# Second norm and its transposes moved, tile by tile, into the output product's second pass; the feed-forward opens with four half column tiles

## What is computed

```python
def rms_norm(x, g):
    y = x * rsqrt(mean(x * x, axis=-1, keepdims=True) + EPS)
    return y * g

def reference(x, ...):
    ...                                   # norm, combined projection, two attentions, gates -> merged
    x = x + merged @ w_out                # "output product", 1024 x 1024 x 1024
    h2 = rms_norm(x, g_mlp)               # "second norm"
    x = x + square(relu(h2 @ w_ff1)) @ w_ff2   # "feed-forward" (FF), 1024 -> 4096 -> 1024
    return x
```

## Time and profile before

| | |
|---|---|
| median of 3 runs | 1508.72 us (1506.99 to 1510.85) |
| profiled execution | 1510.88 us, of which its span is 1508.7 us |
| PE busy | 1447.4 us (96%), 7304 matmuls |
| PEld busy | 1209.2 us (80%) |
| DVE, ACT, POOL busy | 532.6, 363.2, 498.7 us |
| mean granted TensorE clock | 0.982 |

### The profile page before, as it was taken

The page is one execution under the profiler, slowest core; times in us unless marked ns, Lnnn a source line. Parts: engine busy times, 40 slices in busy tenths (PEclk is TensorE's granted clock), DMA queues, the critical chain, the costliest instruction groups (busy, mean ns, idle before and its releaser), DMA issues.

```text
span 1508.7 us, 18633 instructions
## 1 busy us (share of the span) xinstructions
PE 1447.4 (96%) x7304; PEld 1209.2 (80%) x7304; DVE 532.6 (35%) x974; ACT 363.2 (24%) x781; POOL 498.7 (33%) x351
## 2 busy tenths in 40 slices
PE   7999999976799999899998999999999999999998
PEld 6998888864488887788887888888888888888887
DVE  5300124078566665545235213222221322222222
ACT  5112120175355554200023102020110202011020
POOL 3331554117143241125405225060522406052320
PEclk9999999988799999999999999999999999999999
DMA  7120211000010000015202102030110203021012
GB/s 226 31 57 15 56 42 49 6 23 1 18 38 2 1 1 29 20 51 181 70 1 70 56 28 84 0 94 18 56 55 28 83 0 97 14 62 49 28 41 97
DMA packets 79285, 70.90 MB, mean 47 GB/s; under 512 B 7808, under 2 KB 70784, under 8 KB 79232
## 3 DMA queue, kind: packets, MB, share of 16 engines
q1 hardware_dynamic: 79088, 69.67, 15.2%
q10 hardware_dynamic: 144, 0.52, 0.1%
HBM read 65.99 MB, written 4.19 MB: 47 GB/s over the span
## 4 chain that ended last, share of the span: by engine, by line
PE 88%; DVE 4%; issue 3%; ACT 2%; POOL 1%; DMA 1%; ACTq 0%; SPq 0%; DVEq 0%; POOLq 0%
PE PS L986 73%; PE PS L1133 4%; PE PS L1179 4%; PE PS L993 2%; PE PS L1095 2%; PE PS L1152 1%; ACT scA L891 1%; DVE uT_lo L1623 1%; PE PS L1097 1%; POOL scA L681 1%; PE PS L1175 1%; PE PS L1159 1%; DVE x_norm L1584 0%; DMA x_in<-in_x 0%; PE PS L1148 0%
## 5 line engine op out<-in xcount | busy, mean ns | idle before, releaser
L571 POOL TENSOR_SCALAR w_hi<-raw 128x1024 fp32r<-128x1024 f32 x64 | 74.3, 1160 | 422.2 <-PE PS L986 412.3
L1623 DVE TENSOR_TENSOR uT_lo<-relu_sq,uT_hi 128x512 fp32r<-128x512 f32 x64 | 93.3, 1494 | 280.6 <-ACT uT_hi L974 280.6
L960 ACT ACTIVATE relu_t<-PS 128x512 f32<-128x512 f32 x64 | 34.8, 595 | 557.7 <-PE PS L986 557.7
L1629 DVE TENSOR_TENSOR xr<-PS,xr 128x1024 f32<-128x1024 f32 x64 | 78.4, 1225 | 245.7 <-PE PS L986 245.7
L573 POOL TENSOR_TENSOR w_lo<-raw,w_hi 128x1024 fp32r<-128x1024 f32 x64 | 158.8, 2482 | 5.3
L986 PE MATMUL PS<-w_hi,uT_hi 128*128 128x512 f32 x512 | 158.6, 391 | 1.7 <-DVE uT_lo L1623 1.7
L986 PE MATMUL PS<-h2T_hi,w_hi 128*128 128x512 f32 x512 | 159.2, 390 | 0.0
L986 PE MATMUL PS<-h2T_lo,w_hi 128*128 128x512 f32 x512 | 159.1, 389 | 0.0
L986 PE MATMUL PS<-h2T_hi,w_lo 128*128 128x512 f32 x512 | 159.0, 389 | 0.0
L986 PE MATMUL PS<-w_lo,uT_hi 128*128 128x512 f32 x512 | 157.9, 390 | 0.0
L986 PE MATMUL PS<-w_hi,uT_lo 128*128 128x512 f32 x512 | 157.7, 390 | 0.0
(11 more groups left out here) (194 smaller groups left out, 2395.4 us busy)
## 6 DMA issues: line engine op xcount, KB each, us to landing
raw<-in_w_ff SPq DMA_DIRECT2D x64, 512.0 KB, 3.7
g_raw<-in_w_in SPq DMA_DIRECT2D x16, 512.0 KB, 3.9
x_in<-in_x SPq DMA_DIRECT2D x8, 512.0 KB, 10.5
raw<-in_w_out SPq DMA_DIRECT2D x8, 512.0 KB, 3.5
xr<-in_x SPq DMA_DIRECT2D x8, 512.0 KB, 7.4
out<-xr SPq DMA_DIRECT2D x8, 512.0 KB, 2.6
z_raw<-in_w_in SPq DMA_DIRECT2D x4, 640.0 KB, 7.8
z_raw<-in_w_in SPq DMA_DIRECT2D x4, 544.0 KB, 4.0
```

What stands on the lines that cost most here:

```text
L571: pool.tensor_scalar(hi_ap, raw_ap, 1.0, 1.0, ALU.mult, ALU.mult).then_inc(hi_done, 1)
L960: act.activation(relu_t[:, cols], PS[:, 2 * (j % 2) + h, :], ACT.Relu).then_inc(relu_ready, 1)
L1623: dve.tensor_tensor(uT_lo[:, j, cols], relu_sq[:, cols], uT_hi[:, j, cols], ALU.subtract).then_inc(uT_ready, 1)
L1629: dve.tensor_tensor(xr[:, t, :], pair(4 + 2 * (t % 2)), xr[:, t, :], ALU.add).then_inc(x3_added, 1)
```

## The change

The second norm and its transposes go tile by tile into the second pass of the output product. After step n of the product, from n = 10 on, PE transposes the normalised tile n - 10 (`x2_transposes`), into banks 6 and 7; the second pass itself uses three pairs (0/1, 2/3, 4/5) in place of four (`out_pair`). Tile 5 follows the last step; tiles 6 and 7 stand inside the FF opening, `ff_begin`. Mean and power are now made for one tile at a time. The gain is multiplied in on DVE together with the normalisation, from `g_mlp_r`, the gain in all 128 rows (a 512 KB broadcast, issued by SP between the residual's loads and the output weights 4 to 7), where it was the scale of the copy out of PSUM. The copies out are `h2T_high` on ACT and `h2T_low` on DVE, two banks a tile, each 128 x 4 x 128, written over the part of `mT_hi`, `mT_lo` that belongs to the tokens just used (listings show them under the name `mT_`). ACT's squares go to `x_norm[:, t]` rather than to a scratch tile, so one squaring no longer waits for the one before. `ff_begin` does column tile 0 for tokens 0 to 511, tiles 6 and 7's transposes, column tile 1 for tokens 0 to 511, then both column tiles for tokens 512 to 1023. The small load of the gain by columns (`g_mlp_c`) at the start is gone.

```diff
@@ -369,6 +368,18 @@
             return t if c else t % 2
+        def out_pair(n):
+            return 2 * (n % 4) if n < T else 2 * ((n - 13) % 3)
+        def out_before(n):
+            return max([m for m in range(n) if out_pair(m) == out_pair(n)], default=None)
+        def x2_bank(t, a):
+            return (4 if t == T - 1 else 6) + a
         def bcast(ap, shape):
             return ap.to_broadcast(shape)
...
@@ -526,6 +536,8 @@
             sp.wait_ge(branch_done, 2 * KD)
             for t in range(T):
                 sp.dma_start(xr[:, t, :], x_d[t]).then_inc(xr_landed[t], 16)
+            sp.wait_ge(mT_ready, KD)
+            sp.dma_start(g_mlp_r[:, :], g_mlp[0:1, :].partition_broadcast(P)).then_inc(g_mlp_in, 16)
             for k in range(4, 8):
                 out_load(k)
...
@@ -741,10 +753,9 @@
                         split(raw[n % 2][:, :], w2_hi[j][:, :], w2_lo[j][:, :], w2_hi_done, 4 * g + j + 1, w2_ready)
                 unit(0, 1, 0)
                 if first:
-                    for h in range(2):
-                        pool.wait_ge(x2_ms_ready, h + 1)
-                        power(x_rstd[:, 4 * h:4 * h + 4], x_ms[:, 4 * h:4 * h + 4], 4, (P, 4)
-                              ).then_inc(x2_rstd_ready, 1)
+                    for t in range(T):
+                        pool.wait_ge(x2_ms_ready, t + 1)
+                        power(x_rstd[:, t:t + 1], x_ms[:, t:t + 1], 1, (P, 1)).then_inc(x2_rstd_ready, 1)
                 unit(1, 1, 1)
                 unit(2, 2, 0)
                 unit(3, 2, 1)
@@ -936,18 +947,22 @@
                 act.activation(mT_hi[:, d, :], merged[:, :], ACT.Copy).then_inc(mT_hi_done, 1)
+            def x2_square(t):
+                act.wait_ge(xr_added, T + t + 1)
+                act.activation(x_norm[:, t, :], xr[:, t, :], ACT.Square, accum_out=x_ss[:, t:t + 1]).then_inc(x2_squared, 1)
+            def h2T_high(t):
+                for a in range(2):
+                    act.wait_ge(x2T_done, 2 * t + a + 1)
+                    act.activation(h2T_hi[:, 4 * a:4 * a + 4, t * P:(t + 1) * P],
+                                   PS[:, x2_bank(t, a), :].rearrange("p (j q) -> p j q", q=P), ACT.Copy
+                                   ).then_inc(h2T_hi_done, 1)
             for t in range(T):
-                act.wait_ge(xr_added, T + t + 1)
-                if t:
-                    act.wait_ge(x2_squared, t)
-                act.activation(sq2[:, :], xr[:, t, :], ACT.Square, accum_out=x_ss[:, t:t + 1]).then_inc(x2_squared, 1)
-            for n in range(2 * KD):
-                h, j = n // KD, n % KD
-                act.wait_ge(x2T_done, n + 1)
-                if n == 0:
-                    act.wait_ge(o_done, 2 * T)
-                act.activation(h2T_hi[:, j, h * HALF:(h + 1) * HALF], PS[:, n % 8, :], ACT.Copy,
-                               scale=g_mlp_c[:, j:j + 1]).then_inc(h2T_hi_done, 1)
+                if t >= 2:
+                    h2T_high(t - 2)
+                x2_square(t)
+            h2T_high(T - 2)
+            h2T_high(T - 1)
             def ff_up(g, first):
...
@@ -1223,53 +1238,68 @@
             peeled(pe, KD // 2, branches)
-            for n in range(2 * T):
+            def out_tile(n):
                 r, t = n // T, n % T
                 if t == 0:
                     pe.wait_ge(mT_ready, 4 * (r + 1))
                 if n < 4:
                     pe.wait_ge(merged_ready, KD - 1 if n < 2 else KD)
-                if n >= 4:
-                    pe.wait_ge(xr_added, n - 3)
+                else:
+                    pe.wait_ge(xr_added, out_before(n) + 1)
                 rows = slice(t * P, (t + 1) * P)
                 for k in range(4 * r, 4 * r + 4):
                     if t == 0:
                         pe.wait_ge(ow_ready, k + 1)
+                    b = out_pair(n)
                     ins = split_products(mT_hi[:, k, rows], mT_lo[:, k, rows], ow_hi[k][:, :], ow_lo[k][:, :],
-                                         [(PS[:, 2 * (n % 4) + h, :], halves[h]) for h in range(2)],
+                                         [(PS[:, b + h, :], halves[h]) for h in range(2)],
                                          k, k == 4 * r, k == 4 * r + 3)
                 ins.then_inc(o_done, 1)
...
+            def x2_transposes(t):
+                pe.wait_ge(x2_normed, t + 1)
+                if t == 0:
+                    pe.wait_ge(xr_added, T)
+                elif t == T - 1:
+                    pe.wait_ge(xr_added, 2 * T)
+                else:
+                    pe.wait_ge(h2T_ready, 2 * t)
+                for a in range(2):
+                    transpose_tiles(x2_bank(t, a), [x_norm[:, t, j * P:(j + 1) * P] for j in range(4 * a, 4 * a + 4)]
+                                    ).then_inc(x2T_done, 1)
+            for n in range(2 * T):
+                out_tile(n)
+                if n >= T + 2:
+                    x2_transposes(n - T - 2)
+            def up_half(g, j, hs, ready=None):
+                pe.wait_ge(w1_ready, 4 * g + j + 1)
+                if ready is not None:
+                    pe.wait_ge(h2T_ready, ready)
+                for k in range(KD):
+                    ins = split_products(w1_hi[j % 2][:, k, :], w1_lo[j % 2][:, k, :], h2T_hi[:, k, :], h2T_lo[:, k, :],
+                                         [(PS[:, 2 * (j % 2) + h, :], halves[h]) for h in hs], k, k == 0, k == KD - 1)
+                return ins
+            def ff_begin():
+                pe.wait_ge(xr_added, 2 * T - 2)
+                up_half(0, 0, (0,), T)
+                x2_transposes(T - 2)
+                x2_transposes(T - 1)
+                pe.wait_ge(xr_added, 2 * T - 1)
+                up_half(0, 1, (0,))
+                up_half(0, 0, (1,), 2 * T).then_inc(up_done, 1)
+                up_half(0, 1, (1,)).then_inc(up_done, 1)
             def ff(g, first):
...
+                if first:
+                    ff_begin()
+                for j in range(2 if first else 0, GROUP):
+                    pe.wait_ge(relu_ready, 8 * g + 2 * j - 2)
+                    up_half(g, j, (0, 1)).then_inc(up_done, 1)
...
@@ -1579,10 +1609,21 @@
             peeled(dve, KD // 2, merge)
             def x2_norm(t):
-                if t % 4 == 0:
-                    dve.wait_ge(x2_rstd_ready, t // 4 + 1)
-                dve.tensor_scalar(x_norm[:, t, :], xr[:, t, :], x_rstd[:, t:t + 1], None, ALU.mult
-                                  ).then_inc(x2_normed, 1)
+                dve.wait_ge(x2_rstd_ready, t + 1)
+                dve.scalar_tensor_tensor(out=x_norm[:, t, :], in0=xr[:, t, :], scalar=x_rstd[:, t:t + 1],
+                                         in1=g_mlp_r[:, :], op0=ALU.mult, op1=ALU.mult).then_inc(x2_normed, 1)
+            def h2T_low(t):
+                for a in range(2):
+                    out = h2T_lo[:, 4 * a:4 * a + 4, t * P:(t + 1) * P]
+                    dve.wait_ge(h2T_hi_done, 2 * t + a + 1)
+                    dve.tensor_tensor(out, PS[:, x2_bank(t, a), :].rearrange("p (j q) -> p j q", q=P),
+                                      h2T_hi[:, 4 * a:4 * a + 4, t * P:(t + 1) * P], ALU.subtract).then_inc(h2T_ready, 1)
+            def x2_mean(t):
+                dve.wait_ge(x2_squared, t + 1)
+                dve.tensor_scalar(x_ms[:, t:t + 1], x_ss[:, t:t + 1], 1.0 / D, EPS, ALU.mult, ALU.add
+                                  ).then_inc(x2_ms_ready, 1)
             for n in range(2 * T):
@@ -1592,25 +1633,19 @@
                     dve.wait_ge(xr_landed[t], 16)
                 else:
                     dve.wait_ge(xr_added, T)
-                dve.tensor_tensor(xr[:, t, :], pair(2 * (n % 4)), xr[:, t, :], ALU.add).then_inc(xr_added, 1)
-                if r == 1 and t % 4 == 3:
-                    h = t // 4
-                    ts = slice(4 * h, 4 * h + 4)
-                    dve.wait_ge(x2_squared, 4 * (h + 1))
-                    dve.tensor_scalar(x_ms[:, ts], x_ss[:, ts], 1.0 / D, EPS, ALU.mult, ALU.add
-                                      ).then_inc(x2_ms_ready, 1)
-                if r == 1 and t in (5, 6):
-                    x2_norm(2 * t - 10)
-                    x2_norm(2 * t - 9)
-            for t in range(4, T):
-                x2_norm(t)
-            for n in range(2 * KD):
-                h, j = n // KD, n % KD
-                cols = slice(h * HALF, (h + 1) * HALF)
-                dve.wait_ge(h2T_hi_done, n + 1)
-                dve.scalar_tensor_tensor(out=h2T_lo[:, j, cols], in0=PS[:, n % 8, :], scalar=g_mlp_c[:, j:j + 1],
-                                         in1=h2T_hi[:, j, cols], op0=ALU.mult, op1=ALU.subtract
-                                         ).then_inc(h2T_ready, 1)
+                b = out_pair(n)
+                dve.tensor_tensor(xr[:, t, :], pair(b), xr[:, t, :], ALU.add).then_inc(xr_added, 1)
+                if r == 1:
+                    if t == 0:
+                        dve.wait_ge(g_mlp_in, 16)
+                    else:
+                        x2_norm(t - 1)
```

(33 more changed lines are left out.)

11 lines of the change are left out of this document (1 added, 10 removed).

## The result

| | before | after |
|---|---|---|
| first comparison, median of 5 runs each | 1508.72 us (1506.79 to 1511.13) | 1497.71 us (1495.93 to 1499.77) |
| ratio, 95% interval | | 0.9927 [0.991, 0.9945] |
| before once more, beside e1 to e4, 23 runs | 1506.25 us (1502.54 to 1510.98) | |
| profiled execution, span | 1510.88, 1508.7 us | 1497.08, 1495.1 us |
| mean granted clock of the profiled execution | 0.982 | 0.992 |

The change made the kernel faster, as forecast (1500.1 us, range 1497.5 to 1504.5), and it stands near the low end of the range. The first comparison gives 11.0 us.

A forecast was written before the change was run, and what follows sets the result against it. PE, holding 88% of the chain, bounds the kernel. Matmuls 21.76, transposes 6.96 and stall 0.95 make 29.67 us against 38.33, so 1508.72 - 8.66 = 1500.1 us; range 1497.5 to 1504.5.

The forecast's parts named there:

- The place: Between output product and FF, PE spends 16.47 us in which no product advances, and the granted clock falls to 0.50.
- The second pass has no hole: Output product's second pass: a period of 6.31 us, low parts ready at 3.75, 2.5 us to spare, so no wait.
- rival D: Second pass: DVE's chain beyond 6.31 us is paid at five blocks, making the kernel slower, 1513.2 us; chance 0.03.
- The meeting of POOL and DVE behind the last step: After the last output step, POOL's weight split meets DVE's norm of tile 7: norm 2.06 us, weights ready at 8.93.
- The stall: FF opening: PE waits 0.95 us for column tile 1's weights, with bounds of 0.1 and 1.7 us.
- The edits at nothing: Gain broadcast, removed small load at the start (0 to -0.5 us), smaller powers and FF column tile 2: taken as 0.
- Rival A: FF opening: transposes do not keep the clock, it stays at half and 3.2 us are lost; 1503.3 us, chance 0.07.
- upper bound of 1.7: FF opening: longest stall before column tile 1, 1.7 us, if the earlier trace's POOL and DVE durations hold unscaled.
- B: Pass and opening: bubbles of 0.2 us a transpose block and 1.5 us for the split; 1503.2 us, chance 0.07.
- C: FF opening without the POOL and DVE collision, plus a gain at the start: 0.85 + 0.5 more, 1498.7 us; chance 0.08.
- E: FF: the gain is given back in full, its groups hanging on an unmoved DMA or split; 1508.7 us, chance 0.05.

The follow-up runs named there:

- e1: The kernel before the change, run again with no edit: 1506.47 us, ratio 1.0001.
- e4: The changed kernel with POOL's split of the second FF weight tile ahead of the last power instead of behind it: 1496.37 us, ratio 0.9934.
- e7: The changed kernel with two more normalisations a step on DVE, written to scratch that nothing reads: 1500.12 us, ratio 0.996.
- e2: The kernel before, with the small load of the gain moved from the start to just ahead of the residual's loads: 1505.99 us, ratio 0.9997.
- e3: The changed kernel with the old small load of the gain put back at the start, read by nothing: 1497.69 us, ratio 0.9949.
- e9: The changed kernel with 64 more transposes of tile 6 in the opening, behind the first half column tile: 1502.51 us in one run.
- e6: The changed kernel with the second half of column tile 0 ahead of the first half of column tile 1: 1498.4 us, ratio 0.9936.
- e10: A second execution of the changed kernel with column tile 0 done whole before column tile 1: 1501.6 us.
- e8: The changed kernel with four more normalisations a step on DVE, written to scratch that nothing reads: 1518.13 us, ratio 1.0072.

## Why the prediction was right, step by step

**The place.** The time was in the hole between the products and in what it did to the clock. Stage -8.4 us, rest 0.0.

**The second pass has no hole.** Right. Step and block are 6.33 to 6.36 us in the chain (5.46 or 5.49, and 0.87) where 6.31 was worked out; from the block of tile 0 (755.14 on PE) to that of tile 5 (786.91) it is 31.77 us for 31.55. These 0.2 us, and 0.05 in the opening (25.37 for 25.32), are what the forecast of 8.66 had over the measured 8.4. DVE's additions, one step of the pass after:

```profile
774.41 1.22 DVE L1637 TENSOR_TENSOR xr<-PS,xr 128x1024 f32<-128x1024 f32 x1 [2.69 <-PE PS L1001]
775.55 1.27 DVE L1613 SCALAR_TENSOR_TENSOR x_norm<-xr,x_rstd,g_mlp_r 128x1024 f32<-128x1024 f32 x1
776.74 1.28 DVE L1620 TENSOR_TENSOR mT_lo<-PS,mT_hi 128x512 fp32r<-128x512 f32 x2
```

Each is within 0.02 us of its row of before. The low parts end at 778.02, 2.5 us ahead of the next block of transposes (780.54 on PE), which is the 2.5 us to spare that were worked out. e7 used that up and lost nothing in the pass. That is the direct test of rival D.

**The meeting of POOL and DVE behind the last step.** Right to the size. DVE and POOL after:

```profile
791.45 2.06 DVE L1613 SCALAR_TENSOR_TENSOR x_norm<-xr,x_rstd,g_mlp_r 128x1024 f32<-128x1024 f32 x1 [0.66 <-POOL x_rstd L592]
...
790.86 0.55 POOL L592 TENSOR_TENSOR x_rstd<-x_ms,minus_half 128x1 f32<-128x1 f32 x1 [5.82 <-DVE x_ms L1625]
791.39 1.05 POOL L583 TENSOR_SCALAR w_hi<-raw 128x1024 fp32r<-128x1024 f32 x1
792.52 3.21 POOL L585 TENSOR_TENSOR w_lo<-raw,w_hi 128x1024 fp32r<-128x1024 f32 x1
```

From the end of the product, 786.91: addition 0.20 (forecast 0.20), power 3.95 (4.05), `w_hi` 4.48 (4.57), the normalisation of tile 7 at 4.54 (4.63) for 2.06 us (2.06), weight tile ready at 8.82 (8.93). Scaling by the 0.21 us by which `w_hi` is shorter was the right use of a row that is nearly but not quite the same.

**The stall.** Right to 0.05 us. The listed 0.72 counts from the modelled end of the last transpose, 793.24 + 1.91 = 795.15. By slots of 0.87, as the prediction counted, PE was free at 793.24 + 1.74 = 794.98, and stood for 0.90 us, where 0.95 was taken. e4, which takes the cause away, agrees: 1.0 us less in the stage.

**The edits at nothing.** Removing `g_mlp_c` was costed from 0 to -0.5 us, taken 0; e2 and e3 bear this out. The argument was not quite the right one: the queue is freed for 0.4 us only, since the next load inherits the 3.56. Column tile 2 had no hole, nor had FF.

**Rival A, the clock, was closer than its 7 in 100 said, and for another reason.** Its premise, that PE doing only transposes loses the clock, is wrong: e9. The Trainium skill ("TensorE: Matmul & The Clock Gate", "Part 4: PE-mode transpose") says that the full clock does not engage for transposes, which do not count as busy in the same way; e9's 1.00 over 8.89 us disagrees, and the measurement decides. But the clock was near its edge all the same: a hole of 0.72 us leaves it at 1.00, one of 1.99 us in the same place takes it to 0.50 and adds 1.6 us to the 1.27 by which it is longer (e6, e10). Had the stall come out near the upper bound of 1.7, the price might have been more than the stall. The bounds of the prediction counted it once only.

**Rival D was right as a mechanism and too cheap.** It said that every microsecond past 6.31 of DVE's chain is paid at five blocks, and that 8.9 us would bring the kernel to 1513.2. e8's chain is 3.75 + 4 x 1.2 = 8.55 us, and the run took 1518.13. By the rule of five blocks this chain would cost 5 x (8.55 - 6.31) = 11.2 us; the stage is 19.5 longer. PE waits at all eight blocks: at tiles 1 to 6 for the low parts of the tile before (11.0 us as listed), and at tile 0 (behind step 10) and tile 7 for their own normalisation (1.85 and 1.63). (Tile 7's block goes into banks 4 and 5, so it waits for no low parts.) The second weight tile is late as well, and the clock falls in the opening. The point at which the pass begins to pay lies between e7's 3.75 + 2.4 = 6.15 (no hole) and 8.55.

**B, C and E.** No block had a bubble of more than 0.05 us (B); the meeting happened (C); nothing was given back (E).

**The measured time.** 1497.71 is 2.4 us below the forecast. The stage gained 0.3 less than worked out, so this is no gain of the change: the forecast stood on 1508.72 for before, and 23 runs put that 2.5 us lower. 1506.25 - 8.4 = 1497.85. That the time lies inside the range all the same, 0.2 us above its lower bound, is luck: the bound was drawn for (C), whose gain did not come. What the working itself gets credit for is the stage, 8.4 us for 8.66, with its hole, its meeting and its clock.

## What to carry to other kernels

Work of a second engine that stands between two long products can be cut by tile and laid behind the steps of the first product; it costs no wait as long as its chain is shorter than a step, and the price is then in the tail behind the last step. Work that tail out instruction by instruction from rows in which the same engines already meet. Price a hole on TensorE with what it does to the clock behind it, and cut a profile at two instructions that both kernels have before a difference of spans is laid to the change.
